# A decoder step with 32 experts: weight pieces of 2 MB instead of 1 MB, and other routing and last-pair code

## The chip, the core and the metric

The kernel runs on one core of one Trainium2 chip. All numbers are float32. A core has TensorE (PE, matrix products; PEld is its load of the stationary operand), VectorE (DVE), ScalarE (ACT), GpSimd (POOL) and SyncE (SP), which here only issues DMAs. Sixteen DMA engines serve the queues of the core. The metric is the device time of one launch in microseconds (us).

## What is computed

One layer of a decoder for 256 prompt tokens and 8 x 8 sample tokens, 320 tokens in all, each of 2048 features. A mixing part (a projection, an RWKV-7 recurrence and a retention, in 8 pairs of heads, and an output projection `w_out`) is followed by a mixture of experts: a token's group is chosen out of 4, then 2 of the 8 experts in it.

```python
x = x + concat([y_a, y_b]) @ w_out
h = rmsnorm(x, norm_ffn_g)
grp = argmax(h @ router_coarse)                    # of 4
lf = (h @ router_fine)[grp]                        # 8 logits
top_p, top_i = top_k(softmax(lf), 2)
gates = p_grp * top_p / sum(top_p)
expert = grp * 8 + top_i
out = sum over the two experts of gate * ((silu(h @ w_gate[e]) * (h @ w_up[e])) @ w_down[e])
y = rmsnorm(x + out, norm_final_g)
```

`w_gate` and `w_up` are 2048 x 512 and `w_down` is 512 x 2048 for each of 32 experts: 402.7 MB in all, and every byte is loaded once.

## The kernel before

All engines run code written out by hand, with semaphores; nothing is placed by a scheduler. SBUF is one array `arena`, cut by hand, and it is cut again for the part behind the mixing.

**Mixing.** `schedule` and the strings `PLAN` give the order of each pair's steps. Behind the loop over the pairs, every engine runs the steps that the last pair (7) still owes: the recurrence `r1 a1 s1 ... r3 a3 s3`, in which PE, DVE, PE and ACT take turns, the retention (`oo`, `ms`, `u1`, `u2`), and the norm of the recurrence (`mu`, `va`), at whose end DVE writes the pair's rows of `yT` (`done_y`).

**Output projection.** 16 pieces of `w_out`, 1 MB each, pass through a ring of 8 slots (`wo_piece`, SP). For piece m PE makes 16 matmuls of 320 columns into bank PJ0 or PJ1 in turn (L786); DVE adds the result to `x1T`, the residual, whose first contents SP loads from `xT` when the last pair's outputs are done (L458); PE transposes 128 features of it into banks C0 to C2 (L763), and after each fourth m ACT copies 512 features to `x1`, tokens on partitions, in an order that is turned over (`n (k p) -> n p k`).

**Routing.** PE makes the 36 logits from 16 matmuls (L796), once ACT's copies are done. ACT squares and sums `x1`, DVE divides by the norm, and then 44 small DVE instructions in a row choose group and experts and make the gates, up to `asg_done`. PE makes the ranks of tokens within experts (L806, L808). DVE makes `sc` and the number of rounds `nround`, which every engine reads before its first expert. POOL copies `x1` into `acc` in the mean time (L1671).

**Experts.** Eight quads of four experts. Each quad has room for 32 tokens per expert, and its four experts work side by side in four column strips of the array. The weights come in pieces of 1 MB, 48 to a quad, in a ring of 12 slots (`ex_piece`, `ex_quad`, L481): a slot is loaded again as soon as PE has used its piece (`ex_used`). For q = 0 to 3 PE takes four pieces of gate and four of up (L853, 16 matmuls each), then gathers the tokens of the next quad (`gather(q)`, 12 matmuls, L824: stationary is 128 columns of `x1`, side by side) and adds the outputs of the quad before (`combine(q)`, 3 matmuls, L831). Then come the transposes of the product `hh` (L870, L875) and four groups of four down pieces (L885). Every fp32 matmul stands in the trace as two instructions. A row of a piece is one run of 8 KB in HBM: `(p k) n -> p k n` with k = 4 for gate and up, one row of 2048 for down. In this case's data one round is needed, so the eight quads run once.

**End.** After the last down group ACT copies the outputs, PE and DVE combine four times, and the last norm and the stores follow.

## Time and profile before

| | us |
|---|---|
| median of 3 runs | 2114.92 (2113.86 to 2116.34) |
| profiled execution, its own time | 2114.6 |
| its span in the trace | 2112.8 |
| PE busy | 1722.1 (82%) |
| DVE busy | 614.4 (29%) |
| first expert matmul starts | 1132.12 |
| last expert piece is there | 2067.5 |

The page counts 510.60 MB of DMA. The busy line of the page cuts the span in 40 slices of 52.8 us. Up to about 905 us the pairs are worked off, then come the last pair's rest and the output projection (to 1079), the routing (to 1123), the experts (to 2072) and the end. A clock of 1.00 is 2.4 GHz and 0.50 is 1.2 GHz. A DMA share of 1.01 in a stretch means that all 16 engines were at work throughout.

### The profile page before, as it was taken

Reading aid. Unit: us, or ns where it says so; the run is one execution under the profiler, and the core shown is the slowest. Engines: PE = TensorE matmul, PEld = TensorE weight load, DVE = VectorE, ACT = ScalarE, POOL = GpSimd, SP = SyncE. Lnnn points to the kernel's source line nnn. Section 1 sums busy time; section 2 is a strip of 40 time slices with the busy share of each in tenths; the row PEclk is TensorE's granted clock in tenths of the full one; section 3 lists DMA queues with packets and bytes.
Section 4 is the critical chain, followed back from the end, with each engine's and each line's share of the span. In section 5 each row is a group of like instructions: output and inputs, shape, how many; then the busy total and the mean of one; then the engine's idle time right before and its main releaser. Section 6 shows DMA issues by size and latency. Waiting matters only on the chain.

```text
span 2112.8 us, 26273 instructions
## 1 busy us (share of the span) xinstructions
PE 1722.1 (82%) x9065; PEld 1020.6 (48%) x9065; DVE 614.4 (29%) x1121; ACT 267.7 (13%) x528; POOL 134.9 (6%) x104
## 2 busy tenths in 40 slices
PE   7998989999999999989967867686777767686664
PEld 4776767676776777767734323132222223132111
DVE  6636363635454444430022101111110201111012
ACT  2221212222221212110120000000000000000001
POOL 0202010111102020200020000000000000000000
PEclk9999999999999999989987979798888979798877
DMA  7223222223222312065314999999999999999993
GB/s 269 97 74 108 74 97 79 92 74 107 73 88 67 112 63 97 0 234 219 119 60 180 421 421 421 421 422 422 422 422 422 422 422 422 422 422 422 422 421 112
DMA packets 89261, 510.60 MB, mean 242 GB/s; under 512 B 21376, under 2 KB 24576, under 8 KB 29856
## 3 DMA queue, kind: packets, MB, share of 16 engines
q1 hardware_dynamic: 89136, 509.61, 60.4%
q8 instruction: 29, 0.48, 0.1%
q14 instruction: 48, 0.39, 0.1%
q0 software_dynamic: 48, 0.12, 0.0%
HBM read 499.87 MB, written 9.82 MB: 241 GB/s over the span
## 4 chain that ended last, share of the span: by engine, by line
PE 54%; DMA 26%; DVE 13%; issue 3%; ACT 1%; SPq 1%; DVEq 1%; ACTq 0%
DMA arena<-w_up 15%; PE ps_PJ L567 15%; DVE arena L1158 13%; DMA arena<-w_gate 7%; PE ps_C L853 7%; PE ps_PJ L786 7%; PE ps_PJ L824 4%; DMA arena<-w_down 3%; PE ps_PJ L831 2%; PE ps_C L625 2%; PE ps_C L648 1%; ACT arena L921 1%; SPq L481 1%; PE ps_C L885 1%; PE ps_SB L885 1%
## 5 line engine op out<-in xcount | busy, mean ns | idle before, releaser
L567 PE MATMUL ps_PJ<-arena 128*128 128x320 f32 x1792 | 542.2, 434 | 4.0 <-ACTq L350 4.0
L853 PE MATMUL ps_C<-arena 128*32 128x512 f32 x2048 | 298.2, 736 | 158.5 <-DMA arena<-w_up 123.4
L567 PEld LDWEIGHTS ps_PJ<-arena 128*128 128x128 f32 x1792 | 319.8, 190 | 111.5 <-issue 11.1
L853 PEld LDWEIGHTS ps_C<-arena 128*32 128x32 f32 x2048 | 78.4, 131 | 372.7 <-issue 368.1
L1158 DVE TENSOR_TENSOR arena<-ps_PJ,arena 128x512 f32<-128x512 f32 x32 | 22.1, 692 | 659.2 <-PE ps_PJ L824 659.2
L921 ACT ACTIVATE arena<-ps_C 128x512 f32<-128x512 f32 (+1 forms) x68 | 46.1, 678 | 1152.2 <-PE ps_C L853 621.2
L1158 DVE TENSOR_TENSOR arena<-arena 128x320 f32<-128x320 f32 (+10 forms) x253 | 161.9, 640 | 38.0 <-ACTq L350 15.9
L1609 POOL TENSOR_TENSOR arena<-arena 128x640 f32<-128x640 f32 (+2 forms) x80 | 118.2, 1477 | 786.3 <-DVEq L350 429.1
L1158 DVE TENSOR_TENSOR arena<-arena,ps_PJ 128x512 f32<-128x512 f32 (+2 forms) x112 | 73.5, 656 | 299.4 <-PE ps_PJ L831 166.7
L824 PE MATMUL ps_PJ<-arena 128*128 128x128 f32 (+1 forms) x768 | 140.5, 313 | 3.8 <-DVEq L350 3.8
L786 PE MATMUL ps_PJ<-arena 128*128 128x320 f32 x512 | 142.8, 438 | 0.7 <-issue 0.7
L824 PEld LDWEIGHTS ps_PJ<-arena 128*128 128x128 f32 (+1 forms) x768 | 106.8, 192 | 55.9 <-issue 29.4
L786 PEld LDWEIGHTS ps_PJ<-arena 128*128 128x128 f32 x512 | 97.5, 193 | 40.8 <-issue 3.4
L885 PE MATMUL ps_C<-arena 128*32 128x512 f32 x256 | 48.5, 835 | 78.3 <-DMA arena<-w_down 76.1
L831 PE MATMUL ps_PJ<-arena 128*128 128x512 f32 (+1 forms) x192 | 98.5, 634 | 2.7 <-ACTq L350 2.7
L1158 DVE COPY arena<-ps_C 128x128 f32<-128x128 f32 (+3 forms) x99 | 42.0, 424 | 181.0 <-PE ps_C L657 71.9
L921 ACT ACTIVATE arena<-arena 128x320 f32<-128x320 f32 (+7 forms) x135 | 63.6, 471 | 178.1 <-DVEq L350 77.8
L1158 DVE SCALAR_TENSOR_TENSOR arena<-arena 128x320 f32<-128x320 f32 (+5 forms) x146 | 73.1, 501 | 13.6 <-DVE arena L1158 8.7
L1158 DVE TENSOR_TENSOR arena<-arena,ps_C 128x512 f32<-128x512 f32 x56 | 38.6, 689 | 111.2 <-PE ps_C L648 108.9
L921 ACT ACTIVATE arena<-ps_PJ 128x256 f32<-128x256 f32 (+2 forms) x96 | 36.9, 384 | 223.2 <-PE ps_PJ L567 144.5
L1158 DVE RECIPROCAL arena<-arena 128x320 f32<-128x320 f32 (+1 forms) x29 | 54.5, 1881 | 35.7 <-ACTq L350 33.1
L625 PE MATMUL ps_C<-arena 128*128 128x128 f32 x320 | 43.3, 277 | 16.2 <-DVEq L350 16.2
(175 smaller groups left out, 1374.4 us busy)
## 6 DMA issues: line engine op xcount, KB each, us to landing
arena<-w_gate SPq DMA_DIRECT2D x128, 1024.0 KB, 19.6
arena<-w_up SPq DMA_DIRECT2D x128, 1024.0 KB, 19.0
arena<-w_down SPq DMA_DIRECT2D x128, 1024.0 KB, 18.7
arena<-win SPq DMA_DIRECT2D x59, 1024.0 KB, 4.8
arena<-w_out SPq DMA_DIRECT2D x16, 1024.0 KB, 10.0
arena<-xT SPq DMA_DIRECT2D x8, 640.0 KB, 6.0
arena<-s_ret SPq DMA_DIRECT2D x8, 512.0 KB, 3.8
o_sret<-arena SPq DMA_DIRECT2D x8, 512.0 KB, 3.9
```

What stands on the lines that cost most here:

```text
L481: sp.dma_start(dst, src).then_inc(ex_in[s], 16)
L567: last = mm(pj(j)[:, 0:T], wt[j % NSLOT][:, kt, :], hT[:, kt, :], start=kt == 0, stop=kt == KT - 1)
L625: last = mm(b[:, i * P:(i + 1) * P], Lm[:, k % 2, c, :], V[:, c, :], start=True, stop=True)
L648: last = mm(bank("dv" + k)[:, c * P:(c + 1) * P], U[:, c, :], Z[:, c, :], start=True, stop=True)
L786: last = mm(pj(m)[:, 0:T], w[:, i, :], yT[:, kt, :], start=i == 0, stop=i == KT - 1)
L824: last = mm(XB[b][:, k * P:(k + 1) * P], x1[0:nt, t, kt * P:(kt + 1) * P], pick[0:nt, t, :], start=t == 0, stop=t == 2)
L831: mm(XB[b][0:nt, :], gT[:, t0:t0 + nt], yp[:, n * F:(n + 1) * F], start=True, stop=True).then_inc(x_full[b], 1)
L853: last = mm((GB, UB)[u][h * CAP:(h + 1) * CAP, :], xg[:, kt, h * CAP:(h + 1) * CAP], w[h][:, k, :], start=kt == 0, stop=kt == KT - 1)
L885: last = mm(DB[n][h * CAP:(h + 1) * CAP, :], hhT[:, k, h * CAP:(h + 1) * CAP], w[h][:, n * F:(n + 1) * F], start=k == 0, stop=k == 3)
L921: ins = nc.scalar.activation(*args, **kw)
L1158: ins = build(*args)
L1609: ins = nc.gpsimd.tensor_tensor(*args)
```

## The change

- **Pieces.** A piece of expert weights is 2 MB, 24 to a quad, in a ring of 8 slots (16 MB instead of 12). A partition's run in HBM is 16 KB: k = 8 for gate and up, two rows together for down. PE's groups of four pieces have 32 matmuls instead of 16, and the four slots are given back at the end of the group, in its last four matmuls. Two gathers stand together, and two combines.
- **Gather.** Since a partition now holds eight successive weight rows, gather takes every eighth column of `x1` as the stationary operand (step 32 bytes). `x1` is stored in plain order, and the copy into `acc` is plain too; it is made by ACT instead of POOL. The transposes of `hh` take every second column.
- **Last pair.** 28 of the 32 matmuls of the first two `w_out` pieces (`early`) stand between the last pair's steps. The ring for `w_out` has 5 slots; three pieces are issued during the last pair's projections, and four expert pieces between `w_out` pieces 5 to 8.
- **Routing.** The logits are made in four parts of four matmuls between the pieces of the output projection, even and odd features in two column halves; a matrix `fold` adds the halves. ACT squares each 512 features as they come. Group and expert choice takes 23 DVE instructions up to `asg_done` instead of 44, with the gates made behind it. The number of rounds is made and read off the way to the first expert.

What stands on PE behind the last pair's loop, before; L786 is the output projection, the other rows are the last pair's steps (`a2` is L661, `ms` L736, `s2` L668 to L676, `u1` L740):

```order
L734 MATMUL ps_RT<-arena 128x128 [waits free_RT]
L661 MATMUL ps_C1<-arena 128x128 [waits free_C0,free_C1]
L736 MATMUL ps_RT<-arena 128x320 [waits free_RT]
L668 MATMUL ps_YB<-arena 128x64 [waits free_SB,free_C1,free_C2]
L669 MATMUL ps_YB<-arena 128x64
L670 MATMUL ps_YB<-arena 128x64
L674 MATMUL ps_C2<-arena 128x128
L675 MATMUL ps_C2<-arena 128x128
L676 MATMUL ps_C2<-arena 128x128
L740 MATMUL ps_RT<-arena 128x512 [waits done_vrx,free_RT]
```

The same place on PE after the change; L783 is the output projection:

```order
L752 MATMUL ps_RT<-arena 128x128 [waits free_RT]
L783 MATMUL ps_PJ1<-arena 128x320 x2
L679 MATMUL ps_C1<-arena 128x128 [waits free_C0,free_C1]
L783 MATMUL ps_PJ1<-arena 128x320 x2
L754 MATMUL ps_RT<-arena 128x320 [waits free_RT]
L783 MATMUL ps_PJ1<-arena 128x320 x2
L686 MATMUL ps_YB<-arena 128x64 [waits free_SB,free_C1,free_C2]
L687 MATMUL ps_YB<-arena 128x64
L688 MATMUL ps_YB<-arena 128x64
L692 MATMUL ps_C2<-arena 128x128
L693 MATMUL ps_C2<-arena 128x128
L694 MATMUL ps_C2<-arena 128x128
```

One or two matmuls of the output projection now stand behind every step. In the loop over the quads, PE before, from the second gate group of a quad's end to the down groups:

```order
L824 MATMUL ps_PJ0<-arena 128x128 [waits x_free0]
L824 MATMUL ps_PJ0<-arena 128x128 x11
L831 MATMUL ps_PJ1<-arena 128x512 [waits x_free1]
L815 REGISTER_ALU
L831 MATMUL ps_PJ0<-arena 128x512 [waits x_free0]
L831 MATMUL ps_PJ1<-arena 64x512 [waits x_free1]
L847 REGISTER_ALU
L853 MATMUL ps_C0<-arena 32x512 [waits expert_in2,expert_in1,expert_in3,expert_in0,xg_done]
L853 MATMUL ps_C0<-arena 32x512 x15
L853 MATMUL ps_C1<-arena 32x512 [waits expert_in6,expert_in7,expert_in5,expert_in4]
L853 MATMUL ps_C1<-arena 32x512 x15
L824 MATMUL ps_PJ0<-arena 128x128 [waits x_free0]
```

The same stretch on PE after the change (L895 gate and up, L865 gather, L872 combine):

```order
L895 MATMUL ps_C1<-arena 32x512 [waits expert_in2,expert_in3,expert_in0,expert_in1]
L895 MATMUL ps_C1<-arena 32x512 x31
L865 MATMUL ps_PJ0<-arena 128x128 [waits x_free0]
L865 MATMUL ps_PJ0<-arena 128x128 x11
L865 MATMUL ps_PJ1<-arena 128x128 [waits x_free1]
L865 MATMUL ps_PJ1<-arena 128x128 x11
L856 REGISTER_ALU
L872 MATMUL ps_PJ0<-arena 128x512 [waits x_free0]
L872 MATMUL ps_PJ1<-arena 128x512 [waits x_free1]
L856 REGISTER_ALU
L872 MATMUL ps_PJ0<-arena 64x512 [waits x_free0]
L872 MATMUL ps_PJ1<-arena 128x512 [waits x_free1]
```

A group has twice the matmuls, and two gathers and two combines stand in a row where one of each stood between two pairs of groups. On SP, from the load of `xT` on, before:

```order
L458 DMA arena<-xT 128x1280 [waits out_R2,out_So,out_Rs0,out_S,out_shift,done_ret,done_y]
L458 DMA arena<-xT 128x1280 x3
L459 DMA arena<-router 128x576
L460 DMA arena<-gffn 128x16
L461 DMA arena<-rcst 128x52
L465 DMA arena<-gffn 32x4x1 x16
L481 DMA arena<-w_gate 128x2048 x4
L442 DMA arena<-w_out 128x2048 [waits wo_used] x8
L481 DMA arena<-w_up 128x2048 [waits wo_used] x4
L481 DMA arena<-w_gate 128x2048 [waits wo_used] x4
L481 DMA arena<-w_up 128x2048 [waits expert_used] x4
```

And after the change:

```order
L474 DMA arena<-router 128x16x36 [waits rg_zero]
L475 DMA arena<-gffn 128x16
L476 DMA arena<-rcst 128x52
L480 DMA arena<-gffn 16x8x1 x16
L497 DMA arena<-w_gate 128x4096
L408 DMA arena<-w_out 128x2048 [waits wo_used]
L497 DMA arena<-w_gate 128x4096
L408 DMA arena<-w_out 128x2048 [waits wo_used]
L497 DMA arena<-w_gate 128x4096
L408 DMA arena<-w_out 128x2048 [waits wo_used]
L497 DMA arena<-w_gate 128x4096
L408 DMA arena<-w_out 128x2048 [waits wo_used] x8
```

Four expert pieces, each of 2 MB, now stand between pieces of `w_out`, and the other four of the first eight behind `w_out`'s last.

The core of the diff:

```diff
-PIECES = QUAD * 12
+PIECES = QUAD * 6
 KORD = [*range(7), *range(8, 15), 7, 15]
-NSLOT_B, NSLOT_C = 8, 12
+NSLOT_B, NSLOT_C = 5, 8
+WSLOT = [2, 3, 4, 0, 1]
+BIGSLOT = 2 * SLOT
+ESLOT = [4, 5, 6, 7, 1, 0, 2, 3]
...
                 load_ret(q)
+                if not more:
+                    for m in range(3):
+                        sp.wait_ge(used, tile_no(q, 2 + m) + 1)
+                        wo_piece(m)
...
             def ex_piece(i, c, it):
 
-                s = (c + NSLOT_B) % NSLOT_C
-                dst = arena[:, s * SLOT:(s + 1) * SLOT]
+                s = ESLOT[c % NSLOT_C]
+                dst = arena[:, experts_at + s * BIGSLOT:experts_at + (s + 1) * BIGSLOT]
                 h = c % QUAD
-                if c < 8 * QUAD:
+                if c < 4 * QUAD:
                     q, u = c // (2 * QUAD), c // QUAD % 2
                     w = (w_gate, w_up)[u]
-                    src = w[QUAD * i + h, q * F:(q + 1) * F, :].rearrange("(p k) n -> p k n", k=4)
-                    dst = dst.rearrange("p (k n) -> p k n", k=4)
+                    src = w[QUAD * i + h, q * 2 * F:(q + 1) * 2 * F, :].rearrange("(p k) n -> p k n", k=8)
+                    dst = dst.rearrange("p (k n) -> p k n", k=8)
                 else:
-                    k = c // QUAD - 8
-                    src = w_down[QUAD * i + h, k * P:(k + 1) * P, :]
+                    k = c // QUAD - 4
+                    src = w_down[QUAD * i + h, 2 * k * P:2 * (k + 1) * P, :].rearrange("(p j) n -> p j n", j=2)
+                    dst = dst.rearrange("p (j n) -> p j n", j=2)
                 sp.dma_start(dst, src).then_inc(ex_in[s], 16)
...
-            for c in range(4):
-                ex_piece(0, c, 0)
-            for m in range(NSLOT_B, 2 * NSLOT_B):
+            for m in range(NSLOT_B, KT):
+                if m - NSLOT_B < 4:
+                    ex_piece(0, m - NSLOT_B, 0)
                 sp.wait_ge(wo_used, m - NSLOT_B + 1)
                 wo_piece(m)
-            for c in range(4, PIECES):
-                if c >= NSLOT_C:
-                    sp.wait_ge(ex_used, c - NSLOT_C + 1)
-                else:
-                    sp.wait_ge(wo_used, NSLOT_B + c - 4 + 1)
+            sp.wait_ge(wo_used, KT - NSLOT_B + 2)
+            ex_piece(0, 4, 0)
+            sp.wait_ge(wo_used, KT)
+            for c in range(5, NSLOT_C):
+                ex_piece(0, c, 0)
+            for c in range(NSLOT_C, PIECES):
+                sp.wait_ge(ex_used, c - NSLOT_C + 1)
                 ex_piece(0, c, 0)
...
+            early = [(m, i) for m in range(2) for i in range(KT - 2)]
+            wait_done(pe, "y", PAIRS - 2)
+            wait_done(pe, "ret", PAIRS - 2)
+            for it in schedule(False, True):
+                if it[0] == "step":
+                    step(PAIRS - it[2], it[1])
+                    if it[1] in bank_of:
+                        for _ in range(2 if it[1][0] in "aresm" else 1):
+                            if early:
+                                out_proj(*early.pop(0))
...
+            def logits(g):
+
+                if g == 0:
+                    pe.wait_ge(named["rg_done"], 1)
+                for k in range(4 * g, 4 * g + 4):
+                    h = k % 2
+                    last = mm(LB[64 * h:64 * h + 64, 0:T], rg[:, k, :], x1T[:, k, :], start=k < 2, stop=k >= KT - 2)
+                if g == 3:
+                    last.then_inc(named["lgT_full"], 1)
...
-                    kt = 4 * q + k
+                    at = q // 2 * 2 * F + 4 * (q % 2) + k
                     for t, (t0, nt) in enumerate(TT_):
-                        last = mm(XB[b][:, k * P:(k + 1) * P], x1[0:nt, t, kt * P:(kt + 1) * P], pick[0:nt, t, :], start=t == 0, stop=t == 2)
+                        last = mm(XB[b][:, k * P:(k + 1) * P], x1[0:nt, t, at:at + 8 * (P - 1) + 1:8], pick[0:nt, t, :], start=t == 0, stop=t == 2)
...
                     for u in range(2):
-                        w = [piece_in(2 * QUAD * q + QUAD * u + h, it).rearrange("p (k n) -> p k n", k=4) for h in range(QUAD)]
-                        for k in range(4):
-                            kt = 4 * q + k
+                        w = [piece_in(2 * QUAD * q + QUAD * u + h, it).rearrange("p (k n) -> p k n", k=8) for h in range(QUAD)]
+                        for k in range(8):
+                            kt = 8 * q + k
                             for h in range(QUAD):
                                 last = mm((GB, UB)[u][h * CAP:(h + 1) * CAP, :], xg[:, kt, h * CAP:(h + 1) * CAP], w[h][:, k, :],
                                           start=kt == 0, stop=kt == KT - 1)
-                                if k == 3:
+                                if k == 7:
                                     last.then_inc(ex_used, 1)
                     if more:
                         if q == 0:
                             pe.wait_ge(named["sel_done"], it + 2)
-                        gather(q, sel)
+                        gather(2 * q, sel)
+                        gather(2 * q + 1, sel)
...
+            round_of_experts(0)
             pe.wait_ge(named["routed"], 1)
-            round_of_experts(0)
...
-                    last = A(x1[0:nt, t, g * F:(g + 1) * F].rearrange("n (k p) -> n p k", k=4),
-                             OB[t][0:nt, :].rearrange("n (p k) -> n p k", k=4), ACT.Copy)
+                    last = A(x1[0:nt, t, g * F:(g + 1) * F], OB[t][0:nt, :], ACT.Copy)
                 last.then_inc(tr_free, 1)
+                if g == 0:
+                    act.wait_ge(named["ss_zero"], 1)
+                for t, (t0, nt) in enumerate(TT_):
+                    last = A(hhT[0:nt, :, :].rearrange("p k n -> p (k n)"), x1[0:nt, t, g * F:(g + 1) * F], ACT.Square, accum_out=ss4[0:nt, t, g:g + 1])
+                if g == 2:
+                    A(rstd[:, 0:1], eps[:, 0:1], ACT.Sqrt)
+            last.then_inc(named["squared"], 1)
             use = Use()
-            act.wait_ge(named["ss_zero"], 1)
-            for t, (t0, nt) in enumerate(TT_):
-                A(yp[0:nt, :], x1[0:nt, t, :], ACT.Square, accum_out=ss[0:nt, t:t + 1])
+            act.wait_ge(named["ss_done"], 1)
             A(rstd, ss, ACT.Sqrt, bias=eps[:, 0:1], scale=1.0 / D).then_inc(named["root_done"], 1)
             act.wait_ge(named["cmax_done"], 1)
             A(q4[:, :, :], q4[:, :, :], ACT.Exp).then_inc(named["cexp_done"], 1)
             act.wait_ge(named["dm_done"], 1)
             A(e2, e2, ACT.Exp).then_inc(named["e2_done"], 1)
+            for t, (t0, nt) in enumerate(TT_):
+                last = A(acc[0:nt, t, :], x1[0:nt, t, :], ACT.Copy)
+            last.then_inc(named["acc_init"], 1)
...
-            for gi in range(NG):
-                src = lg[:, :, NG + gi * EG:NG + (gi + 1) * EG]
-                g1 = goh[:, :, gi:gi + 1].broadcast_to([P, 3, EG])
-                if gi == 0:
-                    TT(lf[:, :, :], src, g1, ALU.mult)
-                else:
-                    TT(q8[:, :, :], src, g1, ALU.mult)
-                    TT(lf[:, :, :], lf[:, :, :], q8[:, :, :], ALU.add)
+            fine = lg[:, :, NG:36].rearrange("p t (g e) -> p t g e", g=NG)
+            by_group = lambda x: x[:, :, :].rearrange("p t (g e) -> p t g e", g=NG)
+            group = goh[:, :, :, None].broadcast_to([P, 3, NG, EG])
+            TT(by_group(asg), fine, group, ALU.mult)
+            RED(lf[:, :, :], asg[:, :, :].rearrange("p t (g e) -> p t e g", g=NG), AX_X, ALU.add)
             RED(m1, lf[:, :, :], AX_X, ALU.max)
             pick(oh1, lf[:, :, :], m1, EG, q8)
             STT(lf2[:, :, :], oh1[:, :, :], -BIG, lf[:, :, :], ALU.mult, ALU.add)
             RED(m2, lf2[:, :, :], AX_X, ALU.max)
+            TT(e2, m2, m1, ALU.subtract).then_inc(named["dm_done"], 1)
             pick(oh2, lf2[:, :, :], m2, EG, q8)
-            TT(e2, m2, m1, ALU.subtract).then_inc(named["dm_done"], 1)
+            TT(lf2[:, :, :], oh1[:, :, :], oh2[:, :, :], ALU.add)
+            TT(by_group(asg), lf2[:, :, None, :].broadcast_to([P, 3, NG, EG]), group, ALU.mult).then_inc(named["asg_done"], 1)
...
+            def rounds_needed():
+                dve.wait_ge(named["total_full"], 1)
+                RED(cmx, LB[:, 0:NE], AX_X, ALU.max)
+                TT(over, cmx.broadcast_to([P, ROUNDS - 1]), caps, ALU.is_gt)
+                RED(cmx, over, AX_X, ALU.add)
+                TSC(nround[:, :], cmx, 1.0, None, ALU.add).then_inc(named["routed"], 1)
```

## Rows read from the trace of the kernel before

**Rows 1.** The page, 40 slices of the span: granted clock in tenths, DMA rate.

```profile
PEclk9999999999999999989987979798888979798877
GB/s 269 97 74 108 74 97 79 92 74 107 73 88 67 112 63 97 0 234 219 119 60 180 421 421 421 421 422 422 422 422 422 422 422 422 422 422 422 422 421 112
```

**Rows 2.** Windows: us, busy of PE, PEld, DVE, ACT, POOL (x), clock, DMA share, GB/s.

```profile
907.50:933.00 25.50, 18.19 (x98) 13.65 (x98) 9.03 (x18) 6.79 (x12) 2.61 (x2) 0.84 0.91 369
1123.70:1131.00 7.30, 7.30 (x24) 5.61 (x24) 2.12 (x4) 0.00 (x0) 0.00 (x0) 0.50 0.01 2
1430.00:1550.00 120.00, 85.96 (x515) 32.15 (x519) 15.02 (x23) 4.02 (x7) 0.00 (x0) 0.87 1.01 422
```

**Rows 3.** Timeline, last pair to output projection: start, us, engine, line, what, count [idle before].

```profile
933.73 19.89 PE L786 MATMUL ps_PJ<-arena 128*128 128x320 f32 x64 [0.71 <-issue]
937.60 1.95 SPq L458 DMA_DIRECT2D arena<-xT  x4
1070.04 8.78 PE L786 MATMUL ps_PJ<-arena 128*128 128x320 f32 x32
1078.93 0.49 DVE L1158 TENSOR_TENSOR arena<-arena,ps_PJ 128x320 f32<-128x320 f32 x1 [8.46 <-PE ps_PJ L786]
```

**Rows 4.** Timeline, the routing.

```profile
1080.12 3.17 ACT L921 ACTIVATE arena<-ps_C 128x512 f32<-128x512 f32 x3 [24.53 <-PE ps_C L763]
1083.40 1.91 ACT L921 ACTIVATE arena<-arena 128x2048 f32<-128x2048 f32 x1
1083.47 11.41 PE L796 MATMUL ps_C<-arena 128*36 128x320 f32 x32 [3.39 <-ACTq L350]
1096.10 10.89 POOL L1671 COPY arena<-arena 128x2048 f32<-128x2048 f32 x3 [184.57 <-PE ps_C L800]
1097.04 9.98 DVE L1158 TENSOR_TENSOR arena<-arena 128x12 f32<-128x12 f32 x3
1107.25 1.91 DVE L1158 TENSOR_TENSOR arena<-arena 128x12 f32<-128x12 f32 x9
```

**Rows 5.** Timeline, the first expert groups.

```profile
1122.29 3.74 DVE L1158 TENSOR_TENSOR arena<-arena 128x384 f32<-128x384 f32 x6 [1.07 <-issue]
1123.64 7.54 PE L824 MATMUL ps_PJ<-arena 128*128 128x128 f32 x24 [3.78 <-DVEq L350]
1132.12 9.27 PE L853 MATMUL ps_C<-arena 128*32 128x512 f32 x64 [0.94 <-DVEq L350]
1137.98 2.10 SPq L481 DMA_DIRECT2D arena<-w_up  x4
```

**Rows 6.** Timeline, one quad in the middle, from its last up group on.

```profile
1430.36 5.20 PE L853 MATMUL ps_C<-arena 128*32 128x512 f32 x32 [4.22 <-DMA arena<-w_up]
1435.49 4.30 PE L824 MATMUL ps_PJ<-arena 128*128 128x128 f32 x24
1439.72 3.04 PE L831 MATMUL ps_PJ<-arena 128*128 128x512 f32 x6
1447.14 1.92 PE L885 MATMUL ps_C<-arena 128*32 128x512 f32 x8 [0.31 <-ACTq L350]
1476.07 0.60 ACT L921 ACTIVATE arena<-ps_C 128x512 f32<-128x512 f32 x1 [28.40 <-PE ps_RT L885]
```

**Rows 7.** Windows with all DMA engines at work: runs of 5, of 8 and of 12 KB.

```profile
941.00:944.00 3.00, 3.00 (x12) 2.09 (x11) 0.00 (x0) 0.00 (x0) 0.00 (x0) 1.00 1.01 418
1600.00:1700.00 100.00, 76.11 (x459) 29.31 (x455) 15.02 (x23) 1.63 (x3) 0.00 (x0) 0.89 1.01 422
18.50:20.50 2.00, 1.36 (x4) 0.34 (x3) 1.54 (x4) 0.86 (x2) 0.00 (x0) 1.00 1.01 428
```

**Rows 8.** The page, DMA issues: KB each, median us from issue to landing.

```profile
arena<-win SPq DMA_DIRECT2D x59, 1024.0 KB, 4.8
```

**Rows 9.** Timeline, the end.

```profile
2067.55 1.12 PE L885 MATMUL ps_C<-arena 128*32 128x512 f32 x8 [4.32 <-DMA arena<-w_down]
2075.59 13.40 PE L831 MATMUL ps_PJ<-arena 128*128 128x512 f32 x24 [2.70 <-ACTq L350]
```

More of the change, by code:

```diff
@@ L1544, in experts @@
                     select(sel, i + 1)
-                for q in range(4):
-                    if opening:
-                        gathered(q)
-                    if more:
-                        gathered(q)
-                    if before:
-                        combined(q)
+                for q in range(2):
+                    for on, done_ in ((opening, gathered), (more, gathered), (before, combined)):
+                        if on:
+                            done_(2 * q)
+                            done_(2 * q + 1)
                 dve.wait_ge(named["tanh_done"], it + 1)
```

213 lines of the change are left out of this document (111 added, 102 removed).

## The prediction, made before the change was run

> **What bounds the kernel now.** I read the page's 40 slices first [rows 1]. From slice 23 to 39 the DMA rate stands at 421 to 422 GB/s without a dent, and a window in the middle shows a DMA share of 1.01 while PE is busy for 85.96 of 120 us [rows 2]. So for 925 us the loading of expert weights sets the pace, and PE waits. Ahead of that, slices 18 to 22 move 60 to 234 GB/s: there the last pair, the output projection and the routing are on the path, and DMA waits. The time is therefore the moment at which the saturated stream starts, plus the bytes not yet in the ring divided by the rate, plus what follows the last landing. The first slots are given back by PE in the first gate group, and SP issues at 1137.98 [rows 5]. The last piece is there at 2067.55 [rows 9]; the end takes 2112.8 - 2067.5 = 45.3 us. I work each of these terms for the changed kernel.
>
> **The last pair.** From 907.5 to 933 PE is busy 18.2 of 25.5 us at a mean clock of 0.84 [rows 2]: it changes turns with DVE and ACT. 28 of the 32 matmuls of pieces 0 and 1 now stand there. One is two instructions; 64 took 19.89 us at a mixed clock and 32 take 8.78 us at the full one [rows 3], the last's end counted, so a matmul is 0.54 us and the 28 are 15.1 us. Only 7.3 us of PE were idle, so at least 7.8 us push the steps behind them, less about 2 us because PE, no longer idle, should keep 2.4 GHz where the mean was 0.84. I take the pair's end 5.7 us later: `xT` is issued at 943.3 instead of 937.60 [rows 3]. Behind it PE has 4 matmuls and then must wait for the first `xT` part (4.5 us to land by my estimate: a 1 MB piece needs 4.8 [rows 8]) and DVE's add of 0.5: piece 2 starts at 948.3. Before, it started when the 64 were done, at 953.6. **Gain 5.3** (2 to 8). Pieces 2 to 15 keep their pace; with 5 slots a piece is issued four pieces ahead, some 35 us for a transfer of 2.5, even behind one of 5.
>
> **Logits and norm.** Three of the four logit parts, 12 matmuls of two instructions, now stand between output pieces: all 32 instructions took 11.41 us [rows 4]. If the two column halves run side by side, as the four strips do, 12 cost 3.3 us, else 6.5; the four strips do run side by side (64 instructions of 512 columns in 9.27 us, against 3.04 for 6 of the full array [rows 5, 6]), so I take **+3.8**. Behind the last add (1078.93 + 0.49 [rows 3]) 17.4 us went until the logits stood scaled at 1096.8: ACT's turned copies 3.17, then L796 with 11.41, copy, transposes, scaling [rows 4]. Now ACT's plain copies (0.60 each [rows 6]) 1.8 us, three squares of 512 (a quarter of 1.91 and overhead, 0.75 each) 2.2 us, root, reciprocal and scaling about 1.8, transposes ahead 0.6: 6.5 us, with PE's part hidden beside it. **Gain 10.9.**
>
> **Choice.** Three DVE instructions of 12 elements took 9.98 us while POOL copied `x1` (10.89 us); nine others took 1.91, so 0.21 each [rows 4]. The copy goes to ACT, which then has nothing until the first tanh: 3 x 1.91 = 5.7 us, hidden. Gain 9.3. Up to `asg_done` stand 23 instructions instead of 44: 21 x 0.21 = 4.4. The matmuls for the totals, half as many as the ranks' own, leave the path (1.4), and so do five small ones on DVE and the read of `nround` (1.1 [rows 5]) ahead of the first selection: 2.1. **Gain 17.2.** The first gather then starts at 1123.64 - 5.3 + 3.8 - 10.9 - 17.2 = 1094.0. Expert pieces 5 to 7 are issued when the projection ends (1077), 6.3 MB or 15 us, and are needed behind 1118: hidden.
>
> **The first groups.** Two gathers stand ahead of the first group instead of one. The first took 7.54 us at a granted clock of 0.50, 1.2 GHz [rows 2, 5], and I see no reason why the second should not: 15.1 + 0.9 for DVE. A group has 64 instructions, and 64 took 9.27 there [rows 5]. Its slots come back only at its end: 1094.0 + 16.0 + 9.3 = 1119.3, where before it was 1137.98. **The stream starts 18.7 us earlier.** The ring then holds 16.8 MB instead of 12.6: 4.2 MB at 421.7 GB/s are **9.9 us less**. What follows is covered: 16.8 MB are issued by 1127, 40 us of stream.
>
> **The rate.** 385.9 MB remain: 915 us at 421.7 GB/s. Runs are 16 KB instead of 8. With all engines at work the trace has 418 GB/s where most runs are 5 KB, 422 at 8 KB, and 428 in 2 us of 12 KB runs [rows 7]. A run of 5120 bytes on one of 16 engines is 196 ns by that, one of 8192 is 311; a straight line through both gives 617 ns for 16384 or 425 GB/s, and the 12 KB window is nearer to it in size. I take 428, between 422 and 431: 901.6 us, **gain 13.7** (0 to 20). By the Trainium skill (DMA: Bandwidth & Descriptors, Where 436 GB/s comes from) the ports end at 435 GB/s; with that the gain could be no more than 28 us. That rate is in no term here.
>
> **A new wait.** A group of 8.4 MB takes 19.6 us. Its slots come back all together, and a group's load can start only when the group two before it is used up. Where two gathers and two combines and the product's chain stand between, PE needs from the landing of the last up group: 9.0 (group after a pause), 2 x 4.23 (gathers), 2 x 3.35 (combines; 13.40 for four [rows 9]), 4.4 (last combine to first down matmul: 1442.76 to 1447.14), 8.6 (down group, twice rows L885) = 37.2 us [rows 5, 6]. Then 2.3 us of latency (4.8 less 2.5 [rows 8]) and 19.6 for the load: 59.1, against 58.8 for three groups of stream. I take a gap of 1.0 us in six quads, since SP issues four pieces in 2.1 us: **+6** (0 to 20). In the other half no such chain stands: 9.0 + 8.5 + 6.7 + 7.2 = 31.4.
>
> **The end.** The last down group has 64 instructions behind the last landing: 9 us instead of 5.2, **+3.8**, and DVE's read of `nround` now stands behind the last combine, **+1**.
>
> **Sum.** -18.7 - 9.9 - 13.7 + 6 + 4.8 = -31.5 us. From the profiled execution's 2114.6 (span 2112.8) that is 2083.1; it lies 0.3 us from the median, so I say 2083.
>
> **Rivals.**
>
> *The gather becomes slow.* This is the one that ends slower. Gather's stationary operand is read every 32 bytes now. The trace has no strided PE read. Its nearest rows lie far apart: POOL's turned copy reads every 128th element at 1.8 ns each (10.89 us for 3 x 2048, with no plain one to set beside it), while ACT's turned copies took 3.17 us for three against 0.60 for one plain [rows 4, 6], 1.76 times. PE's loads lie close to its matmuls in the gather (24 in 4.23 us, 0.176 each), so a slower load shows in full. A gather slower by a share p costs 15.1 p ahead of the first group, and 8.46 p in each of six quads, since the chain above has no room: 66 p. At p = 0.47 the whole gain is gone; at 0.76 the other half of a quad loses 1 us too and the first quad, with four gathers in a row, about 5: 2083 + 50 + 6 + 5 = 2144. At p = 0.2 it is 2096. I take p near 0, because POOL's row is a strided read and ACT's a strided write, and gather is a read; but this is the weakest step. By the Trainium skill (SBUF — State Buffer, Specifications (TRN2)) lines are 16 bytes and need two hits each for full bandwidth; a step of 32 bytes has one, and a load at half speed would be p of 0.2 to 1, or 2096 to 2176. No row here shows it.
>
> *The rate stays.* If a run costs nothing of its own and the 428 is the edge of a short window, 13.7 us are missing, but the new wait shrinks too, as a group takes 19.9: 2083 + 14 - 3 = 2094.
>
> *The groups are too coarse.* If PE falls to 1.2 GHz in the pauses of 8 us ahead of the last up group and stays there through the gathers (7.54 for 4.23 each), the chain is 44 us and each quad loses 7: +36, 2119, no gain. Against it: behind pauses of 4 us the gather ran at full clock [rows 6].
>
> **How the numbers follow.** My forecast (2070 to 2092) has 0.58. The rate stays: 0.12, 2090 to 2098. Gather slower by 0.15 to 0.4, or half of the coarse case: 0.13, 2093 to 2109. About as before: 0.05. Gather slower by over half or the coarse case in full: 0.10, over 2119. Under 2068: 0.02 and some of the forecast. The range 2066 to 2108 leaves out about 0.2. A measurement can tell about 0.2% here, 4.2 us. Faster 0.85, same 0.05, slower 0.10.
>
> **What the profile after would show.** First gather near 1094 and first expert issue near 1119; a step of the DMA rate from 422 to about 428 in the slices; a gather's 24 instructions in 4.2 us (8 would be the first rival); short dents in the DMA share, one in each quad, behind the down group. Wrong would be: a clock of 0.5 over the gathers, a last pair that ends later than 945, or a DMA share under 0.98 in the middle.

## The result: 1.35% slower, and the profile after

The changed kernel takes 2142.65 us (median of 4 runs, 2141.98 to 2144.28), the kernel before 2114.39 beside it: a ratio of 1.0135, 95% interval 1.0117 to 1.0152. The forecast was 2083 with a range of 2066 to 2108. The profiled execution has a span of 2142.2 us.

The page of the changed kernel, slices of 53.6 us as in [rows 1], then two groups of its costliest instructions: the gather is line 865 now (busy us, mean ns of one | idle before).

```profile
PEclk9999999999999999999967768777776877778686
GB/s 257 103 73 106 74 105 73 88 82 94 73 106 73 106 72 87 41 112 319 93 118 338 429 429 373 416 396 392 412 364 430 400 396 413 365 406 389 430 427 77
...
L865 PE MATMUL ps_PJ<-arena 128*128 128x128 f32 (+1 forms) x768 | 252.0, 477 | 0.4 <-DVEq L361 0.4
...
L865 PEld LDWEIGHTS ps_PJ<-arena 128*128 128x128 f32 (+1 forms) x768 | 201.5, 326 | 58.4 <-issue 48.6
```

Two things are seen. The rate reaches 429 to 430 GB/s, more than the flat 421 to 422 of [rows 1], but only in some slices: between them stand dents down to 364. And a gather load takes 326 ns in the mean. One quad of the stream, PE's timeline (start, us, engine, line, what, count [idle before]), answers to [rows 6]:

```profile
1361.32 9.56 PE L895 MATMUL ps_C<-arena 128*32 128x512 f32 x64 [15.65 <-DMA arena<-w_gate]
1380.90 10.01 PE L895 MATMUL ps_C<-arena 128*32 128x512 f32 x64 [10.02 <-DMA arena<-w_up]
1390.84 15.61 PE L865 MATMUL ps_PJ<-arena 128*128 128x128 f32 x48
1406.38 8.06 PE L872 MATMUL ps_PJ<-arena 128*128 128x512 f32 x12
1414.38 13.94 PE L895 MATMUL ps_C<-arena 128*32 128x512 f32 x128
1428.25 15.62 PE L865 MATMUL ps_PJ<-arena 128*128 128x128 f32 x48
1443.79 8.13 PE L872 MATMUL ps_PJ<-arena 128*128 128x512 f32 x12
...
1487.30 9.71 PE L895 MATMUL ps_C<-arena 128*32 128x512 f32 x64 [15.62 <-DMA arena<-w_gate]
```

Two gathers take 15.6 us, where one took 4.30 [rows 6]: 7.8 each, slower by a share of 0.82. Behind them the second half's gate and up groups run as 128 instructions without a pause: the last gate piece had been there since 1400.36, the last up piece came at 1419.94, while PE was still in the gate group. PE was late. From gate group to gate group this quad is 126.0 us; the six from 1236.05 to 1992.64 have a mean of 126.1. Now the other side, SyncE's issues and the rate in 5 us windows (columns as in [rows 2]):

```profile
1390.92 1.83 SPq L497 DMA_DIRECT2D arena<-w_up  x4
1421.46 8.70 SPq L497 DMA_DIRECT2D arena<-w_down  x8
```

```profile
1420.00:1425.00 5.00, 5.00 (x52) 1.54 (x48) 0.00 (x0) 0.00 (x0) 0.00 (x0) 1.00 0.49 161
1425.00:1430.00 5.00, 5.00 (x38) 2.35 (x30) 0.00 (x0) 0.60 (x1) 0.00 (x0) 1.00 1.03 442
...
1460.00:1465.00 5.00, 5.00 (x52) 1.52 (x48) 0.13 (x1) 0.00 (x0) 0.00 (x0) 1.00 0.39 164
```

The dent is the mark of late slots: the ring's last load was issued at 1390.92 and landed at 1419.94, the next could be issued at 1421.46, when the gate group was through, and its first piece was there at 1429.03. So the DMA engines waited for PE, twice a quad (the second dent is at 1460), and PE for them.

The front of the changed kernel, timeline, which answers to [rows 3] and [rows 5]: `xT` on SyncE's queue, output piece 2, the last add, the scaled logits, the first gathers, the first groups, the first issue into returned slots, the first quad's row of four gathers.

```profile
945.89 2.01 SPq L472 DMA_DIRECT2D arena<-xT  x4
951.38 8.78 PE L783 MATMUL ps_PJ<-arena 128*128 128x320 f32 x32
1080.80 0.49 DVE L1211 TENSOR_TENSOR arena<-arena,ps_PJ 128x320 f32<-128x320 f32 x1 [8.46 <-PE ps_PJ L783]
1087.17 0.83 DVE L1211 TENSOR_SCALAR arena<-ps_SB,arena 128x36 f32<-128x36 f32 x3
1098.00 16.27 PE L865 MATMUL ps_PJ<-arena 128*128 128x128 f32 x48 [0.39 <-DVEq L361]
1115.21 16.60 PE L895 MATMUL ps_C<-arena 128*32 128x512 f32 x128 [0.94 <-DVEq L361]
1124.96 3.04 SPq L497 DMA_DIRECT2D arena<-w_gate  x4
1131.74 31.83 PE L865 MATMUL ps_PJ<-arena 128*128 128x128 f32 x96
```

The first gather starts 25.6 us earlier than before, 4.0 later than forecast. Three of the forecast's signs of being wrong are here: a gather of 24 instructions takes 7.8 us, `xT` is issued behind 945, and the DMA share in the middle (1300 to 1900 us) is 0.95.

### The profile page after: what moved, and what is told of

Read it like the earlier page. It is cut to its first block, busy times and chain, and to the rows that moved or that the text cites. A ratio compares the mean times of both kernels' runs of the same rounds, so it can differ in the third digit from the quotient of the medians.

```text
span 2142.2 us, 25604 instructions
## 1 busy us (share of the span) xinstructions
PE 1788.9 (84%) x9068; PEld 1112.8 (52%) x9068; DVE 604.9 (28%) x1113; ACT 270.8 (13%) x550; POOL 124.0 (6%) x101
## 4 chain that ended last, share of the span: by engine, by line
PE 64%; DMA 18%; DVE 12%; issue 3%; ACT 1%; DVEq 1%; SPq 1%; ACTq 0%
DMA arena<-w_up 15%; PE ps_PJ L585 14%; DVE arena L1211 12%; PE ps_PJ L865 10%; PE ps_C L895 8%; PE ps_PJ L783 6%; PE ps_PJ L872 4%; DMA arena<-w_down 3%; PE ps_C L643 2%; PE ps_C L931 1%; PE ps_C L666 1%; PE ps_SB L931 1%; ACT arena L967 1%; PE ps_YB L931 1%; PE ps_RT L931 1%
## 5 line engine op out<-in xcount | busy, mean ns | idle before, releaser
L895 PE MATMUL ps_C<-arena 128*32 128x512 f32 x2048 | 264.8, 678 | 195.8 <-DMA arena<-w_gate 108.6
L895 PEld LDWEIGHTS ps_C<-arena 128*32 128x32 f32 x2048 | 74.0, 123 | 384.8 <-issue 382.4
L865 PE MATMUL ps_PJ<-arena 128*128 128x128 f32 (+1 forms) x768 | 252.0, 477 | 0.4 <-DVEq L361 0.4
L865 PEld LDWEIGHTS ps_PJ<-arena 128*128 128x128 f32 (+1 forms) x768 | 201.5, 326 | 58.4 <-issue 48.6
L967 ACT ACTIVATE arena<-ps_C 128x512 f32<-128x512 f32 (+1 forms) x68 | 40.6, 598 | 1068.7 <-PE ps_C L895 636.2
L1211 DVE TENSOR_TENSOR arena<-arena 128x320 f32<-128x320 f32 (+11 forms) x242 | 150.9, 623 | 39.9 <-ACTq L361 18.4
L783 PE MATMUL ps_PJ<-arena 128*128 128x320 f32 x512 | 145.3, 438 | 4.8 <-DVEq L361 4.8
L872 PE MATMUL ps_PJ<-arena 128*128 128x512 f32 (+1 forms) x192 | 120.9, 764 | 2.7 <-ACTq L361 2.7
L783 PEld LDWEIGHTS ps_PJ<-arena 128*128 128x128 f32 x512 | 96.2, 192 | 44.6 <-issue 9.3
L1211 DVE COPY arena<-ps_C 128x128 f32<-128x128 f32 (+2 forms) x98 | 41.5, 424 | 182.2 <-PE ps_C L675 76.3
L967 ACT ACTIVATE arena<-arena 128x320 f32<-128x320 f32 (+8 forms) x148 | 71.3, 482 | 162.7 <-DVEq L361 61.3
L872 PEld LDWEIGHTS ps_PJ<-arena 128*128 128x128 f32 (+1 forms) x192 | 33.9, 214 | 81.8 <-DVEq L361 62.4
L931 PE MATMUL ps_C<-arena 128*32 128x512 f32 x256 | 41.5, 725 | 20.7 <-DMA arena<-w_down 18.4
```

The source lines that it names most:

```text
L783: last = mm(pj(m)[:, 0:T], w[:, i, :], yT[:, KORD[i], :], start=i == 0, stop=i == KT - 1)
L865: last = mm(XB[b][:, k * P:(k + 1) * P], x1[0:nt, t, at:at + 8 * (P - 1) + 1:8], pick[0:nt, t, :], start=t == 0, stop=t == 2)
L872: mm(XB[b][0:nt, :], gT[:, t0:t0 + nt], yp[:, n * F:(n + 1) * F], start=True, stop=True).then_inc(x_full[b], 1)
L895: last = mm((GB, UB)[u][h * CAP:(h + 1) * CAP, :], xg[:, kt, h * CAP:(h + 1) * CAP], w[h][:, k, :], start=kt == 0, stop=kt == KT - 1)
L931: last = mm(DB[n][h * CAP:(h + 1) * CAP, :], hhT[:, 2 * k + j, h * CAP:(h + 1) * CAP], w[h][:, j, n * F:(n + 1) * F], start=k + j == 0, st ...
L967: ins = nc.scalar.activation(*args, **kw)
```

## The experiments

The theory was that the step of 32 bytes in the gather's stationary operand makes its loads slow, and that this alone took the gain (S). The rival was that groups of 8.4 MB with two gathers and two combines between them, and the low clock in them, cost the time whatever the step (C). Every kernel was compared with the kernel before on the same chip (medians of 2113.31, 2113.57 and 2114.45 us in the three sets).

**The step alone, in the changed kernel.** The edit, for 4 bytes; in the same way every second, fourth and sixteenth element for 8, 16 and 64:

```diff
-                    at = q // 2 * 2 * F + 4 * (q % 2) + k
+                    at = q // 2 * 2 * F + (4 * (q % 2) + k) * P
...
-    x1[0:nt, t, at:at + 8 * (P - 1) + 1:8]
+    x1[0:nt, t, at:at + P]
```

> The changed kernel with one edit: the gather's stationary operand takes 128 elements that lie side by side (4 bytes apart) in place of every eighth (32 bytes). It gathers other features than the weights' order asks for, so its result is another; counts and sizes of all instructions stay. Theory S (the stride of the operand makes the load slow, and this alone lost the forecast gain): a gather load falls from 330 ns to about 190, two gathers (48 instructions) from 15.6 to about 8.6 us, a quad from 126 to about 120 us, and the time is 2075 to 2092 us. Rival C (groups of 8.4 MB with two gathers and two combines between them, and the low clock in them, cost the time whatever the stride): a quad stays at 125 us or more, and the time above 2120 us.

> The changed kernel with the gather's stationary operand in steps of 8 bytes (every second element); other features, another result. Step 4 gave 189 ns for a load and 2087 us, step 16 gave 328 ns and 2134, step 32 gave 334 ns. If any step but 4 makes the load slow, 8 bytes give about 330 ns; if the cost goes with the 16-byte lines per element, 8 bytes touch half as many lines as 16 and give 190 to 260 ns and 2087 to 2110 us.

> The changed kernel with the gather's stationary operand in steps of 16 bytes (every fourth element) instead of 32; other features, another result. If each element outside a run costs the same, whatever the step, a load is about 330 ns as at 32 bytes and the time about 2142 us. If the cost goes with the number of 16-byte or 32-byte lines touched, 16 bytes cost the same as 32 or half of the excess (about 260 ns, some 2105 us).

> The changed kernel with the gather's stationary operand in steps of 64 bytes; other features, another result. Steps of 4 and 8 bytes gave loads of 189 and 196 ns, 16 and 32 bytes 328 and 334. If only lines of 16 bytes with one element each count, 64 bytes give 334 ns again and about 2142 us; if wider steps cost more, the load is above 400 ns and the time above 2160.

These kernels gather other features than the weights' order asks for, so they measure time alone. One row of each, in the order 4, 8, 16, 32 (the changed kernel) and 64 bytes: all loads of line 865, ns min/median/max, first and last start.

```profile
L865 PEld LDWEIGHTS ps_PJ<-arena x768: 182/189/337, 1095.7 to 1893.2; 128*128 128x128 f32 x128, 64*128 64x128 f32 x64
```

```profile
L865 PEld LDWEIGHTS ps_PJ<-arena x768: 189/196/331, 1096.0 to 1895.8; 128*128 128x128 f32 x128, 64*128 64x128 f32 x64
```

```profile
L865 PEld LDWEIGHTS ps_PJ<-arena x768: 305/328/332, 1095.9 to 1940.7; 128*128 128x128 f32 x128, 64*128 64x128 f32 x64
```

```profile
L865 PEld LDWEIGHTS ps_PJ<-arena x768: 308/334/338, 1098.0 to 1948.6; 128*128 128x128 f32 x128, 64*128 64x128 f32 x64
```

```profile
L865 PEld LDWEIGHTS ps_PJ<-arena x768: 287/310/314, 1096.8 to 1933.3; 128*128 128x128 f32 x128, 64*128 64x128 f32 x64
```

| step, bytes | load, median ns | two gathers in the stream, us | time, us | runs |
|---|---|---|---|---|
| 4 | 189 | 8.52 | 2087.55 | 4 |
| 8 | 196 | 8.85 | 2087.41 | 1 |
| 16 | 328 | 15.6 | 2134.11 | 1 |
| 32 | 334 | 15.6 | 2142.65 | 4 |
| 64 | 310 | 14.65 | 2129.35 | 1 |

With step 4 the time is 2087.55 us (0.9874 of before, interval 0.9857 to 0.989): 55 us less than with step 32, in a kernel that is the same otherwise. S stands, and C falls as the explanation of the loss. The cost is a step function: none to be seen in the time at 8 bytes, most of it at 16 (steps 8, 16 and 64 were run once each, which tells near from far, no more). That fits what the Trainium skill states (SBUF — State Buffer, Specifications (TRN2)): lines of 16 bytes, which need two hits each for full bandwidth. The runs agree up to 32 bytes: with two elements of a line in turn (8 bytes) a load took 196 ns, 7 more than side by side, with one (16 bytes) 328. They also show that 64 bytes are 24 ns quicker than 32; this stays unexplained.

**The step alone, in the kernel before.** The start `at` is that of the changed kernel.

```diff
-    x1[0:nt, t, kt * P:(kt + 1) * P]
+    x1[0:nt, t, at:at + 8 * (P - 1) + 1:8]
```

> The kernel before with one edit: the gather's stationary operand takes every eighth element (32 bytes apart). It gathers other features, so its result is another. Pieces of 1 MB, one gather and one combine between groups, everything else as before. Theory S: a gather load rises from 190 to about 330 ns, 24 instructions from 4.3 to about 7.8 us, although nothing else of the change is there. In the stream PE waits 25 of 120 us for weights and four gathers add 14, so most of it hides; the first gather stood at 1.2 GHz with 7.54 us and costs 0.5 more: 2114 to 2125 us. If the load stays at 190 ns, the stride is not the cause by itself.

It took 2142.16 us (1.0138, 1.0121 to 1.0155). The load was 334 ns as expected, but the time rose by 29 us, not by 0 to 11. The windows show where (columns as in [rows 2]; the first row is the kernel before, the others are this one):

```profile
1150.00:1230.00 80.00, 61.33 (x415) 27.27 (x415) 8.06 (x13) 1.63 (x3) 0.00 (x0) 0.89 1.01 421
1150.00:1230.00 80.00, 74.22 (x335) 43.83 (x334) 5.95 (x9) 0.60 (x1) 0.00 (x0) 0.69 0.80 327
1300.00:1500.00 200.00, 172.33 (x855) 75.10 (x854) 27.30 (x42) 6.58 (x12) 0.00 (x0) 0.79 1.00 414
1500.00:1900.00 400.00, 336.44 (x1708) 152.06 (x1708) 47.82 (x73) 13.53 (x24) 0.00 (x0) 0.81 1.01 422
```

From 1500 on the rate is 422 GB/s: with pieces of 1 MB the stream does hide the slow gather, as expected. In the first quad it doesn't. There two gathers stand between each pair of groups (the first quad's own and the next quad's), 15.7 us instead of 8.5; the rate is 327 where the kernel before had 421, and 80 us at 94 GB/s less are 18 us of stream. From 1230 to 1500 us the rate is still 413 to 414, which is some 5 us more. That is 23 of the 24.0 us by which the spans of the two profiles differ; the profiled execution took 2138.6 us, 3.6 less than the median, so a part of the 29 lies outside what it shows. I had priced only the first gather there.

**x1 in the order of the gather.** This keeps the 2 MB pieces and leaves nothing out. ScalarE writes its copies turned over, and turns them back for `acc`:

```diff
+            def turned(t, nt, g):
+                h = x1[0:nt, t, g // 2 * 2 * F:(g // 2 + 1) * 2 * F].rearrange("n (k p) -> n p k", k=8)
+                return h[:, g % 2 * 64:g % 2 * 64 + 64, :]
...
-                    last = A(x1[0:nt, t, g * F:(g + 1) * F], OB[t][0:nt, :], ACT.Copy)
+                    last = A(turned(t, nt, g), OB[t][0:nt, :].rearrange("n (p k) -> n p k", k=8), ACT.Copy)
```

> The changed kernel, with x1 stored in the order of the gather: ScalarE writes its copies from PSUM turned over, the squares read them so, the copy into acc turns them back (six instructions of 1024 columns), and the gather reads 128 elements side by side. Nothing is left out. Theory S: as the kernel whose gather has step 4, plus 1.3 us behind the last add (three turned copies took 3.17 us in the kernel before, 1.85 plain in the changed one) and up to 1 us for the squares: 2077 to 2095 us. Rival C: above 2120 us.

2090.04 us, 0.9884 (0.9867 to 0.99). From the last add to the first gather 19.4 us pass, where the changed kernel takes 16.7: the three copies take 3.20 us instead of 1.85, and each of the three squares, which now read `x1` in steps, 1.06 instead of 0.63. Turning costs 2.7 us on the path. The first gather stands at 1100.32, 2.3 us later than in the changed kernel. Against this kernel the changed one loses 51.8 us of span, and the timelines say where: 8.6 up to the second quad's gate group (at 1236.05, here at 1227.46; counted from the first gather it is 10.9), 40.5 in the six quads that follow (126.1 us each, here 119.4), 2.8 from the last quad's start to the end.

**The new wait.** The turned kernel still has dents (in the quad that begins at 1346.45 one, behind the first down group: 202 GB/s from 1442 to 1445 us), and a rate of 422 GB/s between 1300 and 1900 us with peaks of 431. The edit moves the combines out of the chain that returns the slots, in PE's loop over the two groups `u` of a half:

```diff
                                 if k == 7:
                                     last.then_inc(ex_used, 1)
+                        if before and u == 0:
...
+                            combine(2 * q)
+                            combine(2 * q + 1)
...
                         gather(2 * q + 1, sel)
                     if before:
...
-                        combine(2 * q)
-                        combine(2 * q + 1)
```

> The kernel with x1 turned over (2090.0 us), with one more edit: the two combines of a half stand between its gate group and its up group, where PE waits for weights anyway, and no longer behind the gathers; VectorE takes them in the same order. Nothing is left out. Theory N (what is still missing of the forecast is the new wait of the 2 MB pieces: PE's chain from a group's landing to the slots' return is longer than three groups of stream; the DMA rate of the turned kernel falls to 409 to 416 GB/s in every third slice): the chain loses two combines, 6 us, the dents go, the rate between 1300 and 1900 us rises from 422 to about 428 GB/s, and the time falls by 8 to 13 us, to 2077 to 2082. Rival: the dents come from the writes or from HBM, not from PE's chain, and the time stays within 3 us of 2090.

> The changed kernel with its slow strided gather kept (330 ns a load), and one edit: the two combines of a half stand between its gate group and its up group. Nothing is left out. It asks how the slow gather costs time in the stream. Theory N: not by its busy time (PE waits 25 of 126 us in a quad) but because it stands in PE's chain between a group's landing and the return of its slots, which has no room at 2 MB a piece. Taking the combines (8.0 us a half) out of that chain then gives back 6 to 8 us in each of six quads although the gather is as slow as before: a quad of 118 to 121 us instead of 126, the rate between 1300 and 1900 us up from 400 to 418 to 427 GB/s, the time 2095 to 2110 us. Rival: the strided reads of the operand disturb the weights' landing in the same memory, so the rate stays near 400 GB/s and the time above 2130.

The window from 1300 to 1900 us of the changed kernel, the turned one, the turned one with combines between, and the changed one with combines between:

```profile
1300.00:1900.00 600.00, 452.78 (x2403) 208.04 (x2395) 69.59 (x107) 20.10 (x35) 0.00 (x0) 0.76 0.95 400
```

```profile
1300.00:1900.00 600.00, 406.07 (x2574) 161.10 (x2575) 75.72 (x116) 20.09 (x35) 0.00 (x0) 0.84 0.99 422
```

```profile
1300.00:1900.00 600.00, 428.74 (x2620) 166.97 (x2623) 78.73 (x121) 21.14 (x37) 0.00 (x0) 0.83 1.01 428
```

```profile
1300.00:1900.00 600.00, 485.22 (x2580) 226.31 (x2577) 75.08 (x115) 20.70 (x36) 0.00 (x0) 0.78 1.00 424
```

With the gather fast, the move brings 2090.04 to 2080.77 us (0.9843, 0.9827 to 0.986), and the rate becomes flat at 426 to 429 in every slice of the stream. A quad is 117.5 us, which is 50.3 MB at 428 GB/s. With the gather as slow as before, the same move brings 2142.65 to 2095.91 us (0.9909, 0.9893 to 0.9926): 47 us without touching the cause. So the slow gather cost its time in the stream as a link of the chain from landing to slot, not as busy time: in the changed kernel it took both, the slow gather and a chain without room. The rival of disturbed landings falls as the main cause; the rate is 424, not 428, and what part of the 4 is PE's chain was not tested. What is left of the slow gather then is 15.1 us, this kernel against the one with the fast gather and the same order. Most of that stands in the first quad, which has no combines to move: 138.1 us from the first gather to the second quad's gate group, against 127.3.

**Pieces of 1 MB with all the rest.** Sixteen slots of 1 MB, one gather and one combine between groups as in the kernel before, `x1` turned over; and the same with twelve slots (12 in place of the 16 below):

```diff
-PIECES = QUAD * 6
-NSLOT_B, NSLOT_C = 5, 8
-BIGSLOT = 2 * SLOT
+PIECES = QUAD * 12
+NSLOT_B, NSLOT_C = 5, 16
+BIGSLOT = SLOT
...
-    w[QUAD * i + h, q * 2 * F:(q + 1) * 2 * F, :].rearrange("(p k) n -> p k n", k=8)
+    w[QUAD * i + h, q * F:(q + 1) * F, :].rearrange("(p k) n -> p k n", k=4)
```

> The changed kernel (its last pair, its routing, its ring of 16 MB) with pieces of 1 MB in 16 slots, four weight rows of 8 KB runs, one gather and one combine between groups of 32 instructions a projection as before, and x1 turned over by ScalarE so that the gather reads side by side. Nothing is left out. It takes the rate and the new wait out of the change. From the forecast's terms: stream starts 11 us earlier than in the turned kernel (one gather, 7.5 us, and half a group, 4.6, fewer ahead of the first slots), the end is 3.8 shorter, the rate is 422 GB/s without dents, which is also the mean of the turned kernel with its dents: 2090 - 11 - 4 = 2075, range 2068 to 2084. If the 2 MB pieces are worth something by themselves, it is above 2090.

> The kernel with 1 MB pieces in 16 slots (2080.9 us), with 12 slots, as the kernel before has. Nothing is left out. The ring term of the forecast: 4.2 MB fewer in the ring when the stream starts are 9.9 us at 422 GB/s: 2090 to 2092. What is left against the kernel before (2113.6) is then the last pair and the routing alone, some 22 us. If the larger ring gives nothing, 2081.

2080.86 us (0.9844, 0.9827 to 0.986) with sixteen slots, 2091.6 us (0.9891, 0.9875 to 0.9908) with twelve. SyncE's queue of the sixteen-slot kernel, its first issue into a returned slot, and its rates:

```profile
1113.73 1.99 SPq L496 DMA_DIRECT2D arena<-w_gate  x4
```

```profile
GB/s 265 107 75 110 76 89 75 109 68 96 64 101 83 71 89 93 90 48 243 211 132 259 421 421 421 421 421 421 423 421 422 421 422 422 422 422 422 421 421 107
```

The turned 2 MB kernel has that issue at 1125.45, the one with combines between at 1123.58. So the large pieces start the stream some 10 to 12 us later, and run it at 428 instead of 422 GB/s once the combines are moved; the 2 MB kernel with combines between and this one both come out at 2080.8. Against pieces of 1 MB in as many bytes of slots, the 2 MB pieces are worth nothing in the sum. The four slots more are worth 10.7 us, and the last pair and the routing, which is what twelve slots of 1 MB leave of the change, 23 us.

**The 28 matmuls inside the last pair.**

```diff
-            early = [(m, i) for m in range(2) for i in range(KT - 2)]
+            early = []
...
-                for i in range(KT - 2 if m < 2 else 0, KT):
+                for i in range(KT):
```

> The kernel with x1 turned over (2090.0 us), but the 28 matmuls of output pieces 0 and 1 that stood among the last pair's steps stand behind the pair again, as in the kernel before. Nothing is left out. By the forecast's first term they gain 5.3 us where they stand: 2095, and the issue of xT comes some 6 us earlier than at 945.8. Rival: what they take from the pair equals what they save behind it, and the time stays within 2 us of 2090.

2098.0 us (0.9925, 0.9908 to 0.9942), 8.0 more than with them. This is not quite the old order, and so not quite the test that I meant: the wait for the pair's last results now stands ahead of all 64 instructions. The first row is PE's, of this kernel, with 5.06 us of idleness that the kernel before, with its wait ahead of the 15th matmul, hasn't [rows 3]:

```profile
938.27 19.53 PE L783 MATMUL ps_PJ<-arena 128*128 128x320 f32 x64 [5.06 <-DVEq L361]
```

What the early matmuls gain over the order of the kernel before is read from the start of piece 2, behind the transposes of piece 0: 953.8 there, 951.4 in the changed kernel's profile, which is 2.4 us. But that execution took 2144.28 us, 1.6 more than the median. The last pair's code is the same in nine other profiles here. In eight of them piece 2 starts at 949.1 to 950.2 and `xT` is issued at 943.6 to 944.7; only the turned kernel's is late as well (951.1 and 945.8). The kernel before has 953.1 in its profile with step 32. So the gain lies between 2.4 and 4.7 us, and the rest of the 8.0 undoes the wait. What makes the 2 us between executions stays open.

## Why the prediction was wrong

The step that failed is "I take p near 0, because POOL's row is a strided read and ACT's a strided write, and gather is a read". p was 0.82. Nothing in the trace of before stood for p = 0: POOL's 1.8 ns an element had no plain copy beside it, so it was no evidence that a strided read is cheap, and the other row, ACT's 1.76 times, and the Trainium skill's lines of 16 bytes (SBUF — State Buffer, Specifications (TRN2)) both said slow. They were set aside by an argument about reads and writes that no row bore, and the case got a chance of 0.10. The argument fails by itself too: the turned kernel's squares, strided reads by ACT, took 1.06 us against 0.63.

The rival named the right path, PE's chain without room, but that its 2144 us lies 1.4 from the measured 2142.65 is in part luck. It was worked out for p = 0.76. It charged 15.1 p, 11.5 us, ahead of the first group; there two strided gathers took 16.27 us against 15.06, only 1.2 more, because at a granted clock of 0.50 a plain load takes as long as a strided one (333 and 334 ns, rows below). It charged 8.46 p and 1 more a quad, 7.4 us; 6.7 was measured against the turned kernel, 7.2 against the one with step 4. What made up for it: the first quad behind its first gathers lost some 10 us and not 5, and the sum without the rival was 4.5 us too low.

Without that step the sum holds to a few us: with a gather of step 4 the changed kernel takes 2087.6, against 2083.

| step of the sum | forecast | measured |
|---|---|---|
| output piece 2 starts | 948.3 | 951.4 (949.1 to 950.2 in eight other profiles) |
| last add to scaled logits | 6.5 us | 6.7 us (1081.3 to 1088.0) |
| first gather | 1094.0 | 1098.0 |
| first slots back | 1119.3 | 1124.96 |
| ring of 16.8 MB | 9.9 us | 10.7 us (12 against 16 slots) |
| rate without dents | 428 GB/s | 428 GB/s |
| new wait at 2 MB | 6 us | 9.3 us (combines between or not) |
| last landing to the end | 45.3 + 4.8 us | 47.8 us (turned kernel, 2042.57 to 2090.4) |

**Right:** the ring, the logits and the choice, and the rate. That the rate came out is in part luck: it was taken from a window of 2 us [rows 7], and in the kernel before, whose stream runs at 422, windows of 2 us show 414 to 430. Its gain was also added a little too high, since 915 less 901.6 us is 13.4, not 13.7. **Mis-sized:** the last pair's term, 2.4 us in the profiled pair instead of 5.3: `xT` was issued 8.3 us later than before, not 5.7, and of the 4.0 us by which the first gather came late 3.1 stood there already at piece 2. The eight other profiles have `xT` within 1.4 us of the forecast's 943.3, so much of this miss belongs to that execution. Also mis-sized is the new wait, for which I had 6 and named the mechanism; its chain and the place of its dent were right, and 6 us out of it removed the dents. **Did not come:** the rival of 1.2 GHz through the gathers; with the fast gather they ran at 1.00 and took 8.52 us for two in all quads of the stream. 2087.6 lies in the band of 2070 to 2092 that the forecast's own case was given.

**What wasn't weighed:** what the larger pieces cost ahead of the stream against their rate. The forecast had both, 15.1 instead of 7.5 us of gathers and 9.3 instead of some 4.6 for the group, but only inside the sum, so it wasn't seen that the change minus its 2 MB pieces would do as well.

## What to carry to other kernels

Before a stationary operand is given a step, look at what the step does within 16 bytes: for fp32, a step of 8 bytes cost nothing in the time here, a step of 16 or 32 made the load 1.74 or 1.77 times as long, and in a run of short matmuls (128 columns) the load is the pace. If a layout has to be turned, turn it once (here in ScalarE's copy from PSUM, 2.7 us on the path with the squares that read it), not in each of the 768 loads that read it. And in a stream from a ring, add up PE's chain from a group's landing to its slots' return: whatever in it can stand where PE waits anyway belongs there.
